# The values' transpose in a decoder layer: VectorE, the output in HBM and ScalarE's queue instead of TensorE

## The reference

```python
h = rms_norm(xp, norm_g[l])
u, gp, q, k, v, ga = split_proj(h, w_in[l])          # one projection, 2048 -> 6144
pm, pbuf = pool_mix(u, zero_buf, 0, pool_w[l], pool_scale[l])
a = dilated_attn_prompt(q, k, v, slopes)             # 16 heads of 64, three patterns
xp = xp + merge_out(pm, gp, a, ga, w_out[l], xp.dtype)
y_prompt = rms_norm(xp, final_norm_g)
# outputs too: k and v of the prompt, [512, 16, 64] each, and the same for the samples
```

## Time and profile before

| | us |
|---|---|
| median of 3 runs | 822.56 |
| lowest, highest | 821.51, 828.95 |
| the profiled execution | 821.09 |
| its span, first to last instruction | 819.3 |
| TensorE busy | 807.1 |
| VectorE busy | 627.4 |
| ScalarE busy | 398.9 |
| GpSimd busy | 203.2 |

### The profile page before, as it was taken

One profiled execution on the slowest core, in us unless ns is written; L12 is line 12 of the kernel. 1 busy time (PEld: TensorE's weight loads), 2 busy tenths in 40 slices (PEclk: granted clock), 3 DMA queues, 4 the chain that ended last, 5 costly groups with the idle time before them and its releaser, 6 DMA issues.

```text
span 819.3 us, 17483 instructions
## 1 busy us (share of the span) xinstructions
PE 807.1 (99%) x6625; PEld 802.6 (98%) x6625; DVE 627.4 (77%) x1347; ACT 398.9 (49%) x875; POOL 203.2 (25%) x340
## 2 busy tenths in 40 slices
PE   9999999999999999999999999999999999999995
PEld 8999999999999999999999999999999999999994
DVE  4657895897589778958885897689888886777765
ACT  4745435533554454345435533553465345555554
POOL 2103502520360045014402610450000131222220
PEclk9999999999999999999999999999999999999998
DMA  8569647856774696578558756884668567766565
GB/s 297 142 173 232 168 125 171 231 144 168 188 208 122 163 233 169 152 175 228 152 141 186 204 147 182 193 214 123 172 195 272 156 181 203 207 184 174 150 180 218
DMA packets 271499, 150.04 MB, mean 183 GB/s; under 512 B 44448, under 2 KB 261472, under 8 KB 271392
## 3 DMA queue, kind: packets, MB, share of 16 engines
q1 hardware_dynamic: 239784, 118.97, 53.7%
q0 software_dynamic: 12672, 20.59, 9.9%
q10 hardware_dynamic: 18960, 9.38, 4.0%
HBM read 119.49 MB, written 28.27 MB: 180 GB/s over the span
## 4 chain that ended last, share of the span: by engine, by line
PE 87%; DVE 6%; DMA 3%; issue 1%; ACT 1%; SPq 1%; POOL 1%; DVEq 0%; ACTq 0%
PE pj L889 64%; PE pj L1048 13%; PE ps_s L946 1%; PE ps_s L948 1%; PE ps_o L977 1%; PE ps_o L975 1%; DMA out<-arena 1%; PE ps_o L889 1%; DVE w_lo L1624 1%; PE ps_t L995 1%; PE ps_s L995 1%; PE ps_s L889 1%; PE ps_s L827 1%; DVE arena L1755 1%; DMA w_raw<-in_w_out 0%
## 5 line engine op out<-in xcount | busy, mean ns | idle before, releaser
L889 PE MATMUL pj<-mov_hi,w_hi 128*128 128x260 f32 (+1 forms) x1632 | 332.1, 285 | 0.3 <-DVE mov_lo L1645 0.3
L889 PE MATMUL pj<-mov_hi,w_lo 128*128 128x260 f32 (+1 forms) x1632 | 328.3, 283 | 0.0
L889 PE MATMUL pj<-mov_lo,w_hi 128*128 128x260 f32 (+1 forms) x1632 | 327.8, 282 | 0.0
L889 PEld LDWEIGHTS pj<-mov_hi,w_hi 128*128 128x128 f32 x1632 | 252.7, 189 | 2.1 <-issue 0.6
L889 PEld LDWEIGHTS pj<-mov_lo,w_hi 128*128 128x128 f32 x1632 | 251.4, 188 | 0.0
L889 PEld LDWEIGHTS pj<-mov_hi,w_lo 128*128 128x128 f32 x1632 | 251.4, 188 | 0.0
L1148 ACT ACTIVATE w_hi<-w_raw 128x640 fp32r<-128x640 f32 (+1 forms) x157 | 121.4, 773 | 228.5 <-PE pj L889 159.3
L1624 DVE TENSOR_TENSOR w_lo<-w_raw,w_hi 128x640 fp32r<-128x640 f32 (+1 forms) x157 | 135.5, 863 | 62.7 <-ACT w_hi L1148 62.3
L1566 POOL DMA_DIRECT2D p_scratch<-extra x168 | 104.8, 631 | 82.4 <-DVE extra L1727 79.9
L1597 POOL DMA_DIRECT2D y_scratch<-arena x56 | 37.6, 678 | 110.5 <-DVE arena L2209 81.3
L1540 POOL DMA_DIRECT2D out<-arena x8 | 4.6, 569 | 213.0 <-DMA arena<-arena 213.0
(11 more groups left out here) (275 smaller groups left out, 1295.3 us busy)
## 6 DMA issues: line engine op xcount, KB each, us to landing
w_raw<-in_w_in SPq DMA_DIRECT2D x96, 320.0 KB, 4.1
w_raw<-in_w_in SPq DMA_DIRECT2D x48, 384.0 KB, 4.5
arena<-in_cache_k_win SPq DMA_DIRECT2D x16, 384.0 KB
arena<-in_cache_v_win SPq DMA_DIRECT2D x16, 384.0 KB
p_scratch<-extra POOLq DMA_DIRECT2D x112, 48.0 KB, 3.3
w_raw<-in_w_out SPq DMA_DIRECT2D x26, 192.0 KB, 3.0
arena<-in_cache_k_win SPq DMA_DIRECT2D x8, 512.0 KB
arena<-in_cache_v_win SPq DMA_DIRECT2D x8, 512.0 KB
```

The costliest lines, as they stand in the source:

```text
L889: mm = pe.matmul(dst[h][:, 0:own.stop - own.start], w, m[:, k, own], start=(k == 0 and i == 0), stop=(c == 2 and k == KT - 1 and i == 2))
```

## The change

For pairs one to seven the values take a way like that of the keys and the probabilities.

- VectorE transposes `z_v` in 32x32 blocks at step 9, late part, into the tile of the turned keys, which is now shared and called `kv_sq`. The last pair is left as it was.
- SP stores the blocks at step 12 with four DMAs into the output `v_win_p`, where they are in their final place. The store at step 14 is gone.
- ScalarE waits at step 13, early part, until the four stores have landed (semaphore `kv_st`), and its queue fetches the 128 columns of the pair back from the output into `v_nat`.
- The high and low part of the values are made at step 14 instead of 12, behind the landing of the fetch (`v_nat_c`, which counts 16 for a DMA).
- The keys' transpose waits until the values' stores have read `kv_sq`.
- TensorE's four transposes, its waits for `tile_out` and `v_nat_c` at step 10, and ScalarE's copy from `ps_m` are gone.

```diff
@@ SP
-                    if j == 14:
-                        sp.wait_ge(v_nat_c, pr + 1)
+                    if j == 12 and p is not FINAL:
+                        sp.wait_ge(v_nat_t, pr + 1)
+                        for a in range(SQS):
+                            at = P * pr + SQ * a
+                            sp.dma_start(v_sq_out[:, :, at:at + SQ],
+                                         kv_sq[SQ * a:SQ * a + SQ, :].rearrange(
+                                             "p (c x) -> p c x", x=SQ)).then_inc(kv_st, 16)
+                    if j == 14 and p is FINAL:
+                        sp.wait_ge(v_nat_c, 16 * SENT + 1)
...
@@ TensorE
                 if j == 10:
-                    pe.wait_ge(tile_out, 6 * pr + 5)
+                    if p is FINAL:
+                        pe.wait_ge(tile_out, 6 * pr + 5)
                     if pr > 0:
-                        pe.wait_ge(v_nat_c, pr)
...
-                    for t in range(QT):
-                        tr = turn(ps_m[:, P * t:P * t + P], z_v[:, P * t:P * t + P])
-                    tr.then_inc(v_nat_t, 1)
+                    if p is FINAL:
+                        for t in range(QT):
+                            tr = turn(ps_m[:, P * t:P * t + P], z_v[:, P * t:P * t + P])
+                        tr.then_inc(v_nat_t, 1)
...
@@ ScalarE, early
                 if j == 11:
-                    act.wait_ge(v_nat_t, pr + 1)
-                    act.activation(v_nat, ps_m[:, :], ACT.Copy).then_inc(v_nat_c, 1)
+                    if p is FINAL:
+                        act.wait_ge(v_nat_t, pr + 1)
+                        act.activation(v_nat, ps_m[:, :], ACT.Copy).then_inc(v_nat_c, 1)
...
+                if j == 13 and p is not FINAL:
+                    act.wait_ge(kv_st, KV_ST * pr + 16 * SQS)
+                    act.dma_start(v_nat.rearrange("p (t x) -> p t x", t=QT),
+                                  v_out[:, :, P * pr:P * pr + P]).then_inc(v_nat_c, 16)
...
@@ ScalarE, late
-                if j == 12:
-                    act.wait_ge(v_nat_c, pr + 1)
+                if j == (12 if p is FINAL else 14):
+                    act.wait_ge(v_nat_c, 16 * min(pr + 1, SENT) + (p is FINAL))
...
@@ VectorE, late
-                if j == 12:
+                if j == (12 if p is FINAL else 14):
                     dve.wait_ge(v_hi_done, pr + 1)
...
+                if j == 9 and p is not FINAL:
+                    dve.wait_ge(tile_out, 6 * pr + 5)
+                    if pr > 0:
+                        dve.wait_ge(kv_st, KV_ST * pr)
+                    dve.transpose(kv_sq, z_v[:, 0:SEQ]).then_inc(v_nat_t, 1)
...
                 if j == p.kn:
-                    if pr > 0:
-                        dve.wait_ge(kv_st, KV_ST * pr)
-                    dve.transpose(k_sq, z_k[:, 0:SEQ]).then_inc(k_turned, 1)
+                    dve.wait_ge(kv_st, KV_ST * pr + (0 if p is FINAL else 16 * SQS))
+                    dve.transpose(kv_sq, z_k[:, 0:SEQ]).then_inc(k_turned, 1)
```

More of the change, by code:

```diff
@@ L38 @@
 Y_ST = 16 * SQS
[L39 removed]
+KV_ST = 16 * 2 * SQS
 PARTS = P // NB
@@ L279, in layer_step @@
         t16 = take(16)
-        u_sq, k_sq = take(2 * SQ), take(SEQ)
+        u_sq, kv_sq = take(2 * SQ), take(SEQ)
         mix_in = [kk[:, NT * i:NT * i + NT] for i in range(5)] + [z_q]
```

13 lines of the change are left out of this document (7 added, 6 removed).

## The result

The changed kernel took 862.6 us (median of 4 runs, 862.0 to 865.1) beside 822.5 us for the kernel before (821.5 to 829.0). The ratio is 1.048, with an interval of 1.044 to 1.051: slower by 4.8%, about 40 us. The prediction had said 836 us, with a range of 822 to 850. Its direction held; the size did not, and the time lies above its range.

The account below looks back on a forecast made before the run. TensorE, busy 99% without a hole, was taken to bound the kernel. Stalls of 10.5 and 6.9 us less 2.5 us of saved turns gave +14.9 us on the profiled 821.09 us: 836.0 us, range 822 to 850.

Parts of the forecast that it names:

- The bound and the slack: TensorE, busy 99%, runs its queue without a hole; 1.5 us slack before the second score unit of head two.
- first stalls: TensorE waits for VectorE's late bias before head two's second score unit; 0 to 3.35 us a pair, sum 10.5 us.
- VectorE's lateness: How late VectorE starts chunk 15's low part, behind ScalarE's wait for the stores; 0.63 to 4.85 us a pair.
- What is removed: TensorE's four value transposes in each of seven pairs leave its queue: gain 2.5 us, at most 4.2 us.
- VectorE's turn: VectorE's added 128x512 transpose at step 9, 0.70 us, hidden by its next wait for scores; costed at nothing.
- the 4.9 us of the rival: Rival: VectorE's transposes uncovered while the stores are covered, 7 x 0.7 us, giving 823.5 us; chance 0.05.
- The landing, X: Time from the start of the four stores to the last one's landing: 6.1 us, ends 4.3 and 7.6 us.
- a page's fixed cost of 2.0 us: Skill page's fixed cost per DMA, mostly last write's receipt; would make the stores' landing 4.4 us, the sum 827 us.
- The start of the stores, T: The four stores on SP begin when chunk 16's load began in the trace of before; 298.23 us in pair four.
- The rival of an SP that is late in every pair: Rival: SP as late in all pairs as in pair one; 31.9 us of stalls, 850.5 us; chance 0.10.
- What is late next: Chunk 16's load issued some 3 us later behind the stores; TensorE needs it only after its scores; costed at nothing.
- The second stall: Values' split moved to step 14 makes VectorE's next bias some 2.2 us later against 2.5 us slack; sum 6.9 us.

Follow-up runs that it names:

- e11: Kernel before with one more VectorE transpose (128x512) at step 9 of pairs one to seven; 825.0 us, ratio 1.001 (0.998 to 1.004).
- e1: The changed kernel once more, unaltered, for a second profile; 860.8 us, single execution.
- e9: Changed kernel without the four value stores, ScalarE's wait and fetch, values used unturned, keys' transpose moved from step 13 to 16; 833.9 us, single execution.
- e10: Changed kernel without the four value stores, ScalarE's wait and fetch, values used unturned, keys' transpose at step 13; 829.6 us, ratio 1.007 (1.004 to 1.011).
- e13: Kernel before, values stored by four 64 KB stores (128-byte runs) at SP's step 12 instead of one at step 14; 843.5 us, ratio 1.025 (1.020 to 1.029).
- e12: Kernel before with the values' split into high and low part at step 14 instead of 12, pairs one to seven; 828.9 us, ratio 1.007 (1.004 to 1.009).
- e5: Kernel before with VectorE held up by seven more keys' transposes at step 13 of pairs one to seven; 863.8 us, single execution.
- e6: Kernel before with VectorE's seven extra transposes at step 13, plus 36 useless TensorE products where it would wait; 851.6 us, single execution.
- e2: Changed kernel without ScalarE's wait for the value stores and without the fetch, values used unturned; stores and VectorE's transpose stay; 852.2 us, single execution.
- e3: Changed kernel without ScalarE's wait and fetch, values used unturned, keys' transpose moved from step 13 to 16, value stores kept; 859.3 us, single execution.
- e16: Kernel before, with GpSimd issuing four 64 KB value stores (128-byte runs) behind the new key row, replacing SP's one; 839.6 us, ratio 1.021 (1.016 to 1.026).
- e15: Kernel before, with the value store cut into four of 64 KB (128-byte runs) in place at SP's step 14; 823.5 us, ratio 1.000 (0.998 to 1.002).
- e7: Kernel before with VectorE held up by four more transposes at step 13 of pairs one to seven; 838.7 us, single execution.

## Why the prediction missed

**The bound and the slack: right.** The prediction gave TensorE 1.5 us of slack ahead of the second score unit of head two. The seven first stalls are shorter than VectorE's lateness by that, 1.5 to 1.7 us: in pair one the low part of chunk 15 starts 7.6 us later than before (81.05 against 73.47 us) and TensorE stalls 6.15 us.

**What is removed and VectorE's turn: not contradicted.** The saved turns were put at 2.5 us; the sum above comes out with it to within 2 us, which is no proof, and no run measures it alone. VectorE's turn was put at nothing, e11 says 0.1% with an interval around nothing (-0.2 to 0.4%), which leaves out the 4.9 us of the rival.

**The landing, X: nearly right.** 6.1 us forecast; in the seven pairs 4.83, 8.38, 6.22, 5.62, 7.24, 5.75 and 6.80 us, mean 6.4, with pair two outside the stated ends of 4.3 and 7.6. In the second trace (e1) the mean is 7.2 us. VectorE's low part starts 1.4 us after the landing in each pair, forecast 1.25. The prediction set a page's fixed cost of 2.0 us beside this and said that no landing is so short. The section that it quotes describes DMAs which GpSimd issues, and the trace of before does have shorter ones, 1.5 us for a small store of GpSimd (L1556) and 1.9 us for a weight load of SP (L677). The stores here are SP's, and the shortest took 2.2 us. Below is their view. It names them for three of ScalarE's seven waits; in all seven ScalarE starts 0.5 us after the landing:

```profile
L750 SPq DMA_DIRECT2D out<-arena x28: 452/682/1577, 74.8 to 565.7; - x28
...
  ACT w_hi L1158: 33.2, 3
...
DMA to landing us min/median/max: 2.2/3.7/5.6
```

**The start of the stores, T: the first step that failed.** "They begin when the load of chunk 16 begins in the trace of before; call it T." T was read as a constant of each pair. Counted from TensorE's start of chunk 12 the stores begin after 9.2, 4.5, 2.2, 3.1, 4.9, 3.0 and 5.9 us in the changed kernel, 32.8 us in all; the load of chunk 16 begins in the trace of before after 5.1, 4.3, 0.9, 4.8, 1.1, 1.7 and 3.2, 21.1 us in all. SP itself had come later. VectorE's lateness d became 34 us over the seven pairs instead of 19.5, and the first stalls 23.3 us instead of 10.5. Of the 11.7 us by which SP came later some 4 are scatter, since the one trace that the prediction had was an early one (21.0 beside 24.6 and 28.5). Some 7 are left by the means (31.4 beside 24.7); two and three traces are too few to put them down to the change. The rival of an SP that is late in every pair was put at 0.10 with the right remark that SP's lateness is no constant. By which of the moved steps SP comes late ahead of the stores isn't settled; kernels with no stores of the values at all have it too (e9 35.4 us, e10 29.6).

**"What is late next": the second step that failed.** The prediction named the load of chunk 16, some 3 us later behind the stores (3.8 us measured), and took nothing for it, because TensorE needs chunk 16 only after its scores. But the scores hang on VectorE, and VectorE has the low part of chunk 16 ahead of the next bias and waits there for ScalarE, as the rows of e13 show (317.47 and 320.28 us). The stores alone (e13) cost 18 us, on a term that the sum put at nothing. Of TensorE's waits there 7.7 us lie at the score units of head two, by this step; 6.2 us more lie at the values' products, a wait that the traces of before have too, once each at most, and how the stores bring more of it I did not follow. The rule that the prediction used for the wait it did cost (name what is queued behind the waiting instruction) would have found it.

**The second stall: right in size by luck, right in part as a cause.** 6.9 us forecast over all seven pairs, 1.67 + 1.92 + 2.50 = 6.1 us seen, in three pairs where the first stall was some 1 us or less and no half-clock stretch came before it. In the second trace it is 0.3 us in all. That a stretch at half clock gives VectorE time to catch up fits nearly all pairs (in pair five of the second trace there was none, and the second stall was 0.3 us all the same) and wasn't tested. e12 measures the later split alone at 0.4 to 0.9%, 3 to 8 us. The fetch, which the prediction wanted landed within 5 us, took up to 7.5 us, and ScalarE waited for it 2.5 us in three pairs.

**The clock: missing, the third step.** Nothing in the sum stood for it, 10.2 us in the changed kernel's first trace and 13.5 us in its second. The first trace of before shows the lower level only at its end, and no idle time of TensorE in its body over 0.4 us, so it held no price; e5 and e6 give one.

**The wait of the keys' transpose: missing, and hidden.** It costs nothing while ScalarE waits for the same landing, and 33.3 us of VectorE's time in e2.

How the 40 us divide. Three kernels stand on each other like steps. e10 (TensorE's turns gone, VectorE's turn and the later split in) is 4 us over before. With the four stores and the keys' transpose waiting for them (e2) it is 29 us. With ScalarE's wait and fetch too, the changed kernel, it is 37 (e1) to 40 us. So the stores with that wait bring some 25 us, ScalarE's wait and fetch 8.5 to 10. The stores by themselves cost 18 us in the kernel before (e13) and 27 us in a kernel where nobody waits for them (e3 against e9), so what the wait of the keys' transpose adds isn't measured: it may be 7 us or nothing. The parts are not independent: each holds its own share of half clock, and the waits overlap. e2, e3 and e9 are single executions. The sums of stalls and clock are short of the measured spans by up to 5 us in some kernels (e16: 10.3 + 3.4 against 18.9), which stays open.

## What to carry to other kernels

A transfer that nobody waits for still costs what it makes late behind it in its engine's list: find the load that comes after it, and follow that load to the engine that sets the pace, through every instruction in between. Here the same four stores cost 18 us ahead of a weight load and nothing two steps later. And where TensorE has been without a hole, price a stall of several us at its length and half of that part of the half-clock stretch in which TensorE works again; here that added a third to a half of the stalls' length (10.2 us to 31.4 in the changed kernel, 13.2 to 27.5 in e5).

## What the runs showed of the hardware

- The granted clock fell to 0.5, for 3.4 or 6.8 us, at or within 1.4 us behind 37 of the 38 stalls of 2.83 us and more in all the traces; the one without was of 3.69 us (e5). Of 19 stalls between 1.66 and 2.81 us it fell at ten, the shortest of 1.66 (e16), 1.79 (e15) and 1.94 us (e11), and not at nine, the longest of 2.81 us (e2). At shorter ones it never fell (e7 has six of 1.4 us). Useless products in place of the wait kept it at 1.00 (e6). The runs show no sharp border.
- Four issues of stores in runs of 128 bytes took SP 3.10 us in pair one of the changed kernel and 5.28 us in pair four of e3, and 3.08 us on GpSimd (e16); single ones went from 0.45 to 1.58 us on SP. What makes them longer wasn't looked into.
- The fetch of 256 KB took 2.9 to 7.5 us from issue to landing, median 4.2; in three pairs ScalarE waited for it, 2.5 us in all.
